# Feed-forward products of a two-block transformer kernel: seven quarter-size products for eight, with the weight sums on GpSimd

## The chip, the cores and the metric

The kernel runs on one core of a Trainium2 chip. The metric is the device time of one execution, in microseconds (us); smaller is better. A core has five engines with a queue of instructions each: TensorE (PE in the profile; its weight loads are listed apart as PEld), VectorE (DVE), ScalarE (ACT), GpSimd (POOL) and SyncE (SP), which here issues all DMAs. All data is fp32. Semaphores order the engines.

## The reference, cut to what matters

A first block (a hybrid of a recurrence and attention) is followed by a second block of two layers. Each layer ends with a feed-forward part, and that part alone is changed:

```python
DEPTH_2 = 2; N_META = 16; D_FF = 2816         # D_MODEL = 1024, SEQ = 256
h = concatenate([meta, x])                    # 272 tokens
for l in range(DEPTH_2):
    ...                                       # projections, attention, recurrence, convolution
    h = h + merged @ w_out[l]
    f = rms_norm_2(h, ffn_norm_g[l])
    a = silu(f @ w_ffn_gate[l]) * (f @ w_ffn_up[l])
    h = h + a @ w_ffn_down[l]
return h[:, N_META:]
```

Layer 0 computes 272 tokens in it, layer 1 the 256 that are returned.

## The kernel before, in words

Activations stand transposed: features on the 128 partitions, tokens along the free dimension. A tile of 128 features x 272 tokens is one unit of work. The residual `H` has `KD` = 8 such tiles, the hidden layer `FA` has `FT` = 22.

**Weights** come from DRAM in slots of 1 MB (128 partitions x 2048 numbers) into a ring of `RING` = 4. SP waits in `slot_free` until the slot that stood there has been used, then issues one DMA (`sync_layers`). `LSTREAM` gives the order of the slots of a layer: from `FF_S` = 54 on 22 slots in pairs (a gate slot and an up slot, each with two output tiles of 128 columns for all eight k), then from `DN_S` = 76 on 11 slots of the down matrix (two k tiles for all eight outputs each).

**TensorE** (`tensor_layers`) does 22 rounds, each a gate tile (L617) and an up tile (L625) of eight products with 272 (256) moving columns. PSUM banks 0 and 1 take the gates, 2 and 3 the ups. The first round works on `GH`, which is not yet normed, so that TensorE need not wait for the norm: its sum is taken by one product with ones (L443), ScalarE makes the root, and VectorE scales the results of the first two rounds, and writes the normed `NT` (L1073) for the other rounds. Then come 11 slots of down products (L636), which gather in eight banks over all slots. The last waits, `gate_kept` and `up_kept` at `FT`, stand ahead of the first down product.

**ScalarE** takes silu of a gate bank into `SG` (L818), **VectorE** multiplies it with the up bank into `FA` (L1079), and adds the down banks to `H` (L1082). **GpSimd** has no part in the layers of the second block; its last work is in the first block (L1443, L1456).

In the profile an fp32 product is two pairs of a weight load and a matmul, so that a tile of eight products is listed as x16; in a list of the program's order it is x8.

Each engine has its own queue, written in the program's order; there is no scheduler.

## Time and profile before

| | |
|---|---|
| median of 3 runs | 1852.68 us (1852.0 to 1853.68) |
| span of the profiled execution, first to last instruction | 1851.9 us |
| TensorE busy | 1808.0 us, 98% |
| VectorE, ScalarE, GpSimd busy | 738.4, 482.3, 115.9 us |
| mean granted TensorE clock | 0.988 of full speed |
| DMA | 225.20 MB, 122 GB/s in the mean |
| feed-forward part of layer 0, second product tile to last product | 969.51 to 1208.68 us |
| feed-forward part of layer 1, the same | 1623.58 to 1848.86 us |

The span is what this document reckons with; the median of the runs lies 0.8 us above it. A row of the chain of waits gives the start of a piece, its length, the engine and line on which the time passed, and how many instructions it covers; a row of a timeline gives start, length from the first start to the last end, and count, and in square brackets the idle time before it and what ended it. A row of the grouped view has the count, then busy time and mean duration of one, then idle time.

### The profile page before, as it was taken

The numbers are of one execution on the slowest core, as the hardware profiler recorded it, in microseconds if no ns is written. First come the engines' busy times: TensorE is split into PE (matmuls) and PEld (weight loads), VectorE is DVE, ScalarE is ACT, GpSimd is POOL, SyncE is SP. The second block draws the span as 40 slices with busy tenths as digits, with TensorE's granted clock in tenths as the row PEclk, the third lists the DMA queues.
The fourth block names the chain that finished last, engine by engine and source line by source line (L and its number), as shares of the span: only waits on it lengthen the run. The fifth ranks groups of instructions, "written<-read, shape, count | busy, mean of one in ns | idle before, by whom it ended". The sixth has DMA issues, their size and how long they took to land.

```text
span 1851.9 us, 28212 instructions
## 1 busy us (share of the span) xinstructions
PE 1808.0 (98%) x11966; PEld 1430.8 (77%) x11966; DVE 738.4 (40%) x1599; ACT 482.3 (26%) x1036; POOL 115.9 (6%) x133
## 2 busy tenths in 40 slices
PE   8999998999999999999999999999999999999999
PEld 3344654889877888888878888878888888888888
DVE  1233625556356958574211000048667563110000
ACT  2112236344343135642020000051237321110000
POOL 0000600465100000000000000000000000000000
PEclk9999999799899999999999999999999999999999
DMA  8412310000234434333333334443334334433352
GB/s 313 163 46 68 114 46 1 3 4 4 104 132 155 137 129 143 126 126 114 137 137 136 137 137 159 144 152 137 137 136 140 134 114 159 139 143 150 137 182 91
DMA packets 33213, 225.20 MB, mean 122 GB/s; under 512 B 4672, under 2 KB 6080, under 8 KB 6336
## 3 DMA queue, kind: packets, MB, share of 16 engines
q1 hardware_dynamic: 33088, 223.40, 34.0%
q8 instruction: 95, 1.56, 0.3%
q14 instruction: 30, 0.25, 0.0%
HBM read 222.34 MB, written 1.05 MB: 121 GB/s over the span
## 4 chain that ended last, share of the span: by engine, by line
PE 92%; DVE 3%; ACT 2%; SPq 1%; issue 1%; DVEq 0%; DMA 0%; POOL 0%; ACTq 0%
PE PS L457 25%; PE PS L598 12%; PE PS L1695 9%; PE PS L636 8%; PE PS L625 8%; PE PS L617 8%; PE PS L1201 2%; PE PS L1214 2%; PE PS L1634 2%; PE PS L1788 1%; PE PS L470 1%; PE PS L571 1%; SPq L1602 1%; PE PS L540 1%; PE PS L552 1%
## 5 line engine op out<-in xcount | busy, mean ns | idle before, releaser
L457 PE MATMUL PS<-arena,ring 128*128 128x272 f32 (+1 forms) x2176 | 498.1, 389 | 0.0
L457 PEld LDWEIGHTS PS<-arena,ring 128*128 128x128 f32 x2176 | 411.2, 190 | 77.2 <-issue 1.4
L598 PE MATMUL PS<-arena,ring 128*128 128x272 f32 (+1 forms) x1024 | 229.5, 386 | 2.1 <-DVE arena L1059 2.1
L598 PEld LDWEIGHTS PS<-arena,ring 128*128 128x128 f32 x1024 | 194.2, 190 | 36.0 <-DVE arena L1059 2.9
L851 DVE SCALAR_TENSOR_TENSOR arena<-arena,par 128x272 f32<-128x272 f32 (+1 forms) x480 | 214.8, 488 | 16.4 <-issue 0.9
L617 PE MATMUL PS<-arena,ring 128*128 128x272 f32 (+1 forms) x704 | 163.8, 386 | 0.0
L625 PE MATMUL PS<-arena,ring 128*128 128x272 f32 (+1 forms) x704 | 163.8, 386 | 0.0
L1695 PE MATMUL PS<-arena,ring 128*128 128x512 f32 (+2 forms) x448 | 158.2, 514 | 1.7 <-DVEq L1992 1.7
L636 PE MATMUL PS<-arena,ring 128*128 128x272 f32 (+1 forms) x704 | 157.1, 386 | 1.1 <-issue 1.1
L636 PEld LDWEIGHTS PS<-arena,ring 128*128 128x128 f32 x704 | 133.6, 190 | 24.7 <-issue 1.9
L617 PEld LDWEIGHTS PS<-arena,ring 128*128 128x128 f32 x704 | 133.8, 190 | 22.9
L625 PEld LDWEIGHTS PS<-arena,ring 128*128 128x128 f32 x704 | 133.8, 190 | 22.9
L1695 PEld LDWEIGHTS PS<-arena,ring 128*128 128x128 f32 (+1 forms) x448 | 84.0, 189 | 75.0 <-issue 69.5
L653 ACT ACTIVATE arena<-PS 128x272 f32<-128x272 f32 (+1 forms) x144 | 55.6, 392 | 323.8 <-PE PS L457 313.8
L1079 DVE TENSOR_TENSOR arena<-PS,arena 128x272 f32<-128x272 f32 (+1 forms) x44 | 19.0, 433 | 266.8 <-PE PS L625 266.5
L818 ACT ACTIVATE arena<-PS 128x272 f32<-128x272 f32 (+1 forms) x40 | 15.6, 390 | 268.2 <-PE PS L617 268.2
L1082 DVE TENSOR_TENSOR H<-H,PS 128x272 f32<-128x272 f32 (+1 forms) x16 | 6.9, 430 | 151.4 <-PE PS L636 151.4
L1634 PE MATMUL PS<-ring,smalls 128*2 128x256 f32 x192 | 45.0, 390 | 9.0 <-DMA ring<-stream_dram 9.0
L1456 POOL TENSOR_TENSOR ring<-arena,H 128x256 f32<-128x256 f32 x64 | 45.8, 742 | 87.9 <-ACT arena L1375 87.8
L1214 PE MATMUL PS<-arena,ring 64*64 64x32 f32 x1280 | 50.9, 228 | 0.3 <-issue 0.3
L1214 PEld LDWEIGHTS PS<-arena,ring 64*64 64x64 f32 x1280 | 47.0, 145 | 3.3 <-issue 2.1
L1057 DVE TENSOR_TENSOR arena<-PS,arena 128x272 f32<-128x272 f32 (+1 forms) x32 | 13.9, 433 | 80.3 <-PE PS L598 80.3
(323 smaller groups left out, 1777.4 us busy)
## 6 DMA issues: line engine op xcount, KB each, us to landing
ring<-stream_dram SPq DMA_DIRECT2D x207, 1024.0 KB, 4.8
arena<-x_dram SPq DMA_DIRECT2D x1, 2048.0 KB, 11.5
cst<-const_dram SPq DMA_DIRECT2D x1, 1080.0 KB, 7.6
out_dram<-H SPq DMA_DIRECT2D x4, 256.0 KB, 2.1
cst<-const_dram SPq DMA_DIRECT2D x1, 912.0 KB, 17.2
arena<-stream_dram SPq DMA_DIRECT2D x1, 512.0 KB, 7.1
par<-param_dram SPq DMA_DIRECT2D x2, 177.0 KB, 10.8
c<-const_dram SPq DMA_DIRECT2D x1, 128.0 KB, 2.2
```

The lines of the kernel that those rows point to most:

```text
L457: last = mm(PS[:, (m + f) % 4, nw], lslot(l, n, KD, 256)[:, k, P * f:P * f + P], NT[:, k, nw], start=k == 0, stop=k == KD - 1)
L598: last = mm(PS[:, i % 4, NQ], lslot(l, n, KD, 256)[:, k, P * (i % 2):P * (i % 2) + P], src[:, k, NQ], start=k == 0, stop=k == KD - 1)
L617: last = mm(PS[:, f, NQ], lslot(l, n, KD, 256)[:, k, P * f:P * f + P], src[:, k, NQ], start=k == 0, stop=k == KD - 1)
L625: last = mm(PS[:, 2 + f, NQ], lslot(l, n + 1, KD, 256)[:, k, P * f:P * f + P], src[:, k, NQ], start=k == 0, stop=k == KD - 1)
L636: last = mm(PS[:, f, NQ], w[:, k, P * f:P * f + P], FA[:, 2 * i + k, NQ], start=i == 0 and k == 0, stop=i == FT // 2 - 1 and k == 1)
L653: a(out, PS[:, m % 4, nw] if src is None else src, func, **more).then_inc(L["kept"], 1)
L851: stt(CVG[:, c, NQ], CVA[:, c, j + Q0:j + T2], dw_w[l][:, c, j:j + 1], CVG[:, c, NQ], ALU.mult, ALU.add)
L1201: last = mm(PS[halves(h), 4 * d, 32 * q:32 * q + 32], XL[l - 1][halves(h), d, q, :], columns(ZW[halves(h), n % 2, d, 0, q, :], l, GROWN[d] ...
L1214: last = mm(PS[halves(h), 4 * d, 256 + 32 * q:288 + 32 * q], ZW[halves(h), n % 2, d, 1, q, :], P1[halves(h), d, 32 * q:32 * q + 32], start ...
L1456: tt(XL[l - 1][:, d], AS[:, d], over(level_mask(d, l), 4), ALU.mult).then_inc(S["xl_ready"], 1)
L1634: last = mm(PS[0:2, n % 4, 0:256], SC[:, k, :], weights(n, KD, 256)[:, k, :], start=k == 0, stop=k == KD - 1)
L1695: last = mm(out, weights(n, KD, 256)[:, k, P * f:P * f + rows], HT[:, k, lo:T1], start=k == 0, stop=k == KD - 1)
```

## The change

The feed-forward products, but for the first gate and up pair of tiles, go over to Strassen's scheme in the form with seven products and fifteen sums. A slot is seen as four k pairs x (even, odd k) x (first, second 128 columns): four quarters a11, a12, a21, a22 of 4 x 128 columns each, and the tokens are halved (136 + 136, or 128 + 128). Each of the seven products has four k steps with half the tokens: 28 products of 136 columns for a slot, where 16 of 272 stood.

- GpSimd makes four sums of the quarters of each slot (`weight_sums`, into one of four `WS`): TensorE needs them from the third of the seven products on.
- The sums over tokens: of `NT` by VectorE once per layer (`TN`), of `FA` by GpSimd, a pair of tiles at a time (`TF`).
- ScalarE copies the first product out of PSUM (`CA`), VectorE puts the seven together (`combine`, four instructions), ScalarE takes silu of four gate quarters at once, and VectorE multiplies them with four up quarters into two tiles of `FA` after each second slot.
- 20 slots (`QUADS`) of gate and up, then 12 slots for the down matrix: for each of four pairs of output tiles (`fp`) three slots of 4, 4 and 3 k pairs. Each of those comes by two DMAs of up to 512 KB, whose rows in DRAM are 1 KB long.
- The seven results lie in three banks, and two sets of three banks alternate.

The diff, cut to its core:

```diff
-                elif FF_S <= i < DN_S:
-                    sp.wait_ge(L["up_made"], B["up_made"] + 2 * ((i - FF_S) // 2) + 2)
+                elif FF_S <= i < FF_S + 2:
+                    sp.wait_ge(L["up_made"], B["up_made"] + 2)
+                elif FF_S + 2 <= i < DN_S:
+                    sp.wait_ge(L["quad_part"], B["quad_part"] + 3 * (i - FF_S - 1))
                 elif i >= DN_S:
-                    sp.wait_ge(L["down_used"], B["down_used"] + i - DN_S + 1)
+                    down_wait(sp, l, i - DN_S)
...
+        def regions(nth, n):
+            first, second, third = ((5, 6, 7), (1, 2, 3))[nth % 2]
+            return ([PS[:, first, n * i:n * i + n] for i in range(3)] + [PS[:, second, n * i:n * i + n] for i in range(2)]
+                    + [PS[:, third, n * i:n * i + n] for i in range(2)])
...
+        def down_slot(s):
+            fp, i = divmod(s, 3)
+            return fp, range(4 * i, min(4 * i + 4, FT // 2))
+        def down_wait(engine, l, s):
+            if s % 3 < 2:
+                engine.wait_ge(L["down_used"], BASE[l]["down_used"] + 2 * (s // 3) + s % 3 + 1)
+            else:
+                engine.wait_ge(L["fold_made"], BASE[l]["fold_made"] + s + 1)
+        def quarters(l, n):
+            pairs = 4 if n < DN_S else len(down_slot(n - DN_S)[1])
+            w = lslot(l, n, 4, 2, 2, P)[:, 0:pairs]
+            return w[:, :, 0, 0, :], w[:, :, 1, 0, :], w[:, :, 0, 1, :], w[:, :, 1, 1, :]
...
+                if i < DN_S:
+                    sp.dma_start(ring[:, n % RING, :], w2_h[l, LSTREAM[i]]).then_inc(slot_in[n % RING], 16)
+                else:
+                    fp, ks = down_slot(i - DN_S)
+                    to = ring[:, n % RING, 0:512 * len(ks)].rearrange("p (k e c) -> p k e c", e=2, c=256)
+                    of = w2_h[l, DN_S + ks[0]:DN_S + ks[-1] + 1].rearrange("k p (e c) -> p k e c", e=2)
+                    cols = slice(256 * fp, 256 * fp + 256)
+                    sp.dma_start(to[:, :, 0, :], of[:, :, 0, cols]).then_inc(slot_in[n % RING], 16)
+                    sp.dma_start(to[:, :, 1, :], of[:, :, 1, cols]).then_inc(down_in[n % RING], 16)
...
-            pe.wait_ge(L["gate_kept"], B["gate_kept"] + FT)
-            pe.wait_ge(L["up_kept"], B["up_kept"] + FT)
-
-            for i in range(FT // 2):
-                lslot_wait(pe, l, DN_S + i)
-                w = lslot(l, DN_S + i, 2, D)
-                for f in range(KD):
-                    for k in range(2):
-                        last = mm(PS[:, f, NQ], w[:, k, P * f:P * f + P], FA[:, 2 * i + k, NQ],
-                                  start=i == 0 and k == 0, stop=i == FT // 2 - 1 and k == 1)
-                    if i == FT // 2 - 1:
-                        last.then_inc(L["down_made"], 1)
-                if i < FT // 2 - 1:
+            n0, n1 = token_halves(l)
+            nh = n0.stop - n0.start
+            def products(nth, w, sums, even, odd, ts):
+                a11, a12, _, a22 = w
+                a, c, b, g, e, h, d = regions(nth, nh)
+                return ((a, a11, even, n0), (b, a12, odd, n0), (c, sums[1], ts[1], None), (g, sums[0], ts[0], None),
+                        (e, sums[2], ts[2], None), (h, sums[3], odd, n1), (d, a22, ts[3], None))
+            for j in range(QUADS):
+                n = FF_S + 2 + j
+                lslot_wait(pe, l, n)
+                if j >= 2:
+                    pe.wait_ge(L["quad_read"], B["quad_read"] + j - 1)
+                if j == 0:
+                    pe.wait_ge(L["normed"], B["normed"] + 2 * KD)
+                    pe.wait_ge(L["root"], B["root"] + 2)
+                if j == 1:
+                    pe.wait_ge(L["gate_kept"], B["gate_kept"] + 2)
+                    pe.wait_ge(L["up_kept"], B["up_kept"] + 2)
+                made = products(j, quarters(l, n), [WS[j % 4][:, i] for i in range(4)], NT[:, 0::2, :], NT[:, 1::2, :],
+                                [TN[:, i, :, 0:nh] for i in range(4)])
+                for r, (out, w, src, tokens) in enumerate(made):
+                    if r == 2:
+                        if j == 0:
+                            pe.wait_ge(L["halves_made"], B["halves_made"] + 1)
+                        pe.wait_ge(L["slot_sums"], B["slot_sums"] + j + 1)
+                    for k in range(4):
+                        last = mm(out, w[:, k], src[:, k] if tokens is None else src[:, k, tokens], start=k == 0, stop=k == 3)
+                    if r in (2, 4, 6):
+                        last.then_inc(L["quad_part"], 1)
+            for s in range(DOWNS):
+                fp, ks = down_slot(s)
+                lslot_wait(pe, l, DN_S + s)
+                if fp < 2 and ks[0] == 0:
+                    pe.wait_ge(L["quad_read"], B["quad_read"] + QUADS - 1 + fp)
+                if fp >= 2 and ks[0] == 0:
+                    pe.wait_ge(L["h_added"], B["h_added"] + 2 * (fp - 1))
+                if fp == 0:
+                    pe.wait_ge(L["fa_made"], B["fa_made"] + ks[-1])
+                made = products(fp, quarters(l, DN_S + s), [WS[s % 4][:, i] for i in range(4)], FA[:, 0::2, :],
+                                FA[:, 1::2, :], [TF[:, i, :, 0:nh] for i in range(4)])
+                for r, (out, w, src, tokens) in enumerate(made):
+                    if r == 2:
+                        pe.wait_ge(L["slot_sums"], B["slot_sums"] + QUADS + s + 1)
+                        if fp == 0:
+                            pe.wait_ge(L["fa_halves"], B["fa_halves"] + ks[-1] + 1)
+                    for i, k in enumerate(ks):
+                        last = mm(out, w[:, i], src[:, k] if tokens is None else src[:, k, tokens],
+                                  start=k == 0 and r in (0, 3, 5), stop=k == 10 and r in (2, 4, 6))
+                    if ks[-1] == 10 and r in (2, 4, 6):
+                        last.then_inc(L["fold_made"], 1)
+                if s % 3 < 2:
                     last.then_inc(L["down_used"], 1)
...
+            for j in range(QUADS):
+                act.wait_ge(L["quad_part"], B["quad_part"] + 3 * j + 1)
+                a(CA[:, j % 2, 0:nh], regions(j, nh)[0], ACT.Copy).then_inc(L["quad_copied"], 1)
+                if j % 2 == 0:
+                    act.wait_ge(L["quad_read"], B["quad_read"] + j + 1)
+                    a(SGH[:, :, 0:nh], GR[:, 1:5, 0:nh], ACT.Silu).then_inc(L["silu_kept"], 1)
...
+        def weight_sums(e, w, to):
+            a11, a12, a21, a22 = w
+            to = to[:, :, 0:a11.shape[1]]
+            e.tensor_tensor(to[:, 0], a21, a22, ALU.add)
+            e.tensor_tensor(to[:, 2], a11, a21, ALU.subtract)
+            e.drain()
+            e.tensor_tensor(to[:, 1], to[:, 0], a11, ALU.subtract)
+            e.drain()
+            return e.tensor_tensor(to[:, 3], a12, to[:, 1], ALU.subtract)
+        def token_sums(e, even, odd, to, n0, n1):
+            nh = n0.stop - n0.start
+            to = to[..., 0:nh]
+            e.tensor_tensor(to[:, 0], even[..., n1], even[..., n0], ALU.subtract)
+            e.tensor_tensor(to[:, 2], odd[..., n1], even[..., n1], ALU.subtract)
+            e.drain()
+            e.tensor_tensor(to[:, 1], odd[..., n1], to[:, 0], ALU.subtract)
+            e.drain()
+            return e.tensor_tensor(to[:, 3], odd[..., n0], to[:, 1], ALU.subtract)
...
+                    dr()
+                    x = NT.rearrange("p (k e) t -> p k e t", e=2)
+                    token_sums(v, x[:, :, 0], x[:, :, 1], TN, n0, n1).then_inc(L["halves_made"], 1)
...
+            def combine(nth, to, copied, made):
+                cb, ge, hd = sums_of(nth, nh)
+                to, u = to[:, :, 0:nh], UU[:, :, 0:nh]
+                dr()
+                dve.wait_ge(*copied)
+                tt(to[:, 0:2], cb, over(CA[:, nth % 2, 0:nh], 2), ALU.add)
+                dr()
+                dve.wait_ge(made[0], made[1] + 2)
+                tt(u, ge, over(to[:, 0], 2), ALU.add)
+                dr()
+                tt(to[:, 4], ge[:, 0], u[:, 1], ALU.add)
+                dve.wait_ge(made[0], made[1] + 3)
+                return tt(to[:, 2:4], hd, u, ALU.add)
+            for j in range(QUADS):
+                combine(j, UP if j % 2 else GR, (L["quad_copied"], B["quad_copied"] + j + 1),
+                        (L["quad_part"], B["quad_part"] + 3 * j)).then_inc(L["quad_read"], 1)
+                if j % 2:
                     dr()
-                tt(FA[:, i, NQ], PS[:, 2 + i % 2, NQ], SG[:, i % 2, NQ], ALU.mult).then_inc(L["up_kept"], 1)
-            for f in range(KD):
-                dve.wait_ge(L["down_made"], B["down_made"] + f + 1)
-                tt(H[:, f, NQ], H[:, f, NQ], PS[:, f, NQ], ALU.add).then_inc(L["h_added"], 1)
-
-
+                    dve.wait_ge(L["silu_kept"], B["silu_kept"] + j // 2 + 1)
+                    tt(FA[:, j + 1:j + 3, NQ].rearrange("p f (n t) -> p f n t", n=2),
+                       UP[:, 1:5, 0:nh].rearrange("p (f n) t -> p f n t", f=2),
+                       SGH[:, :, 0:nh].rearrange("p (f n) t -> p f n t", f=2), ALU.mult).then_inc(L["fa_made"], 1)
+            for fp in range(4):
+                combine(fp, GR, (L["fold_copied"], B["fold_copied"] + fp + 1), (L["fold_made"], B["fold_made"] + 3 * fp))
+                dr()
+                for f in range(2):
+                    h = H[:, 2 * fp + f, NQ].rearrange("p (n t) -> p n t", n=2)
+                    tt(h, h, GR[:, 1 + 2 * f:3 + 2 * f, 0:nh], ALU.add).then_inc(L["h_added"], 1)
+        def pool_layers(pool, l):
+            g = nc.gpsimd
+            B = BASE[l]
+            NQ = slice(first_token(l), T2)
+            n0, n1 = token_halves(l)
+            def slot_sums(j):
+                lslot_wait(pool, l, FF_S + 2 + j)
+                if 4 <= j < QUADS + 4:
+                    pool.wait_ge(L["quad_part"], B["quad_part"] + 3 * (j - 3))
+                elif j >= 4:
+                    down_wait(pool, l, j - QUADS - 4)
+                weight_sums(g, quarters(l, FF_S + 2 + j), WS[j % 4]).then_inc(L["slot_sums"], 1)
+            pool.wait_ge(L["gate_made"], B["gate_made"] + 1)
+            for j in range(QUADS + DOWNS):
+                slot_sums(j)
+                if j % 2 and j < QUADS + 2:
+                    p = j // 2
+                    if p:
+                        pool.wait_ge(L["fa_made"], B["fa_made"] + p)
+                    else:
+                        pool.wait_ge(L["up_kept"], B["up_kept"] + 2)
+                    token_sums(g, FA[:, 2 * p, :], FA[:, 2 * p + 1, :], TF[:, :, p], n0, n1).then_inc(L["fa_halves"], 1)
+                    g.drain()
...
```

TensorE's queue, layer 0, from the second round made in the old way on; before (gates L617, ups L625, down L636):

```order
L617 MATMUL PS<-arena,ring 128x272 x8
L625 MATMUL PS<-arena,ring 128x272 x8
L617 MATMUL PS<-arena,ring 128x272 x8
L625 MATMUL PS<-arena,ring 128x272 x8
L617 MATMUL PS<-arena,ring 128x272 x8
L625 MATMUL PS<-arena,ring 128x272 x8
```

And now (L672 and L678 the gate and up tile of the second round, L711 the slots; a weight operand without `ring` is one of GpSimd's sums):

```order
L672 MATMUL PS<-arena,ring 128x272 x8
L678 MATMUL PS<-arena,ring 128x272 x8
L711 MATMUL PS<-arena,ring 128x136 x8
L711 MATMUL PS<-arena 128x136 x16
L711 MATMUL PS<-arena,ring 128x136 x12
L711 MATMUL PS<-arena 128x136 x16
L711 MATMUL PS<-arena,ring 128x136 x12
```

What moved: 28 products of 136 columns stand for 16 of 272 in a slot. Two of the seven products of a slot come from the ring (x8), the next four from the sums (x16), the last from the ring again; x12 is the last of one slot and the first two of the next.

GpSimd's queue, layer 0, two slots and one pair of `FA` tiles (L932 to L937 the four sums over a slot, L943 to L948 over tokens); in the queue before nothing stands here:

```order
L932 TENSOR_TENSOR arena<-ring 128x512
L933 TENSOR_TENSOR arena<-ring 128x512
L935 TENSOR_TENSOR arena<-arena,ring 128x512
L937 TENSOR_TENSOR arena<-ring,arena 128x512
L932 TENSOR_TENSOR arena<-ring 128x512
L933 TENSOR_TENSOR arena<-ring 128x512
L935 TENSOR_TENSOR arena<-arena,ring 128x512
L937 TENSOR_TENSOR arena<-ring,arena 128x512
L943 TENSOR_TENSOR arena<-arena 128x136
L944 TENSOR_TENSOR arena<-arena 128x136
L946 TENSOR_TENSOR arena<-arena 128x136
L948 TENSOR_TENSOR arena<-arena 128x136
```

What moved: this group of twelve comes ten times in a layer (for slots 0 to 19), then the slots of the down matrix follow, with one more token group after the second of them.

VectorE's queue at the start of the feed-forward part of layer 0; before (L1070 scales a gate, L1073 makes `NT`, L1079 makes a tile of `FA`):

```order
L1070 TENSOR_TENSOR arena<-PS,arena 128x272
L1073 TENSOR_TENSOR arena<-arena 128x272 x8
L1077 TENSOR_TENSOR arena<-arena 128x272
L1079 TENSOR_TENSOR arena<-PS,arena 128x272
L1070 TENSOR_TENSOR arena<-PS,arena 128x272
```

And now (L1193 for L1070, L1196 for L1073, L943 to L948 the token sums `TN`):

```order
L1193 TENSOR_TENSOR arena<-PS,arena 128x272
L1196 TENSOR_TENSOR arena<-arena 128x272 x8
L943 TENSOR_TENSOR arena<-arena 128x544
L944 TENSOR_TENSOR arena<-arena 128x544
L946 TENSOR_TENSOR arena<-arena 128x544
L948 TENSOR_TENSOR arena<-arena 128x544
L1202 TENSOR_TENSOR arena<-arena 128x272
L1204 TENSOR_TENSOR arena<-PS,arena 128x272
```

What moved: four instructions of 544 elements stand between the normed tiles and the first tile of `FA`.

## Rows read from the trace of the kernel before

**Rows 1.** The page: busy us (share of the span) and instructions of each engine

```profile
PE 1808.0 (98%) x11966; PEld 1430.8 (77%) x11966; DVE 738.4 (40%) x1599; ACT 482.3 (26%) x1036; POOL 115.9 (6%) x133
```

**Rows 2.** Stretches: length; PE, PEld, DVE, ACT, POOL busy (count); clock, DMA share, GB/s

```profile
969.51:1129.83 160.32, 159.74 (x698) 132.16 (x697) 14.19 (x34) 12.28 (x26) 0.00 (x0) 1.00 0.36 134
1129.83:1208.68 78.85, 78.83 (x344) 65.01 (x343) 3.08 (x7) 5.47 (x13) 0.00 (x0) 1.00 0.44 155
...
1772.64:1848.86 76.22, 76.21 (x352) 66.76 (x352) 2.95 (x7) 0.00 (x0) 0.00 (x0) 1.00 0.38 133
```

**Rows 3.** Chain of waits, feed-forward part: start, length, what, count

```profile
964.76 0.02 issue
...
969.51 3.67 PE PS L625 x16
...
1627.03 3.45 PE PS L617 x16
...
1772.07 0.56 issue
```

**Rows 4.** Chain, products of 144 and of mixed columns; a group of weight loads

```profile
767.73 0.98 PE PS L552 x8
...
836.40 3.98 PE PS L571 x24
...
L571 PEld LDWEIGHTS PS<-arena 128*128 128x128 f32 x96 | 15.3, 190 | 2.4 <-ACT arena L794 1.2
```

**Rows 5.** GpSimd's instructions grouped by shape

```profile
L1443 POOL TENSOR_TENSOR arena<-arena 128x512 f32<-128x512 f32 x16 | 20.0, 1271 | 72.9 <-ACT arena L1123 72.9
...
L1934 POOL TENSOR_TENSOR H<-cst 128x64 f32<-128x64 f32 x12 | 3.4, 321 | 21.4 <-DMA cst<-const_dram 21.4
```

**Rows 6.** Timeline of GpSimd: with a drain between, and back to back

```profile
220.24 2.35 POOL L1954 TENSOR_TENSOR arena<-arena 128x1024 f32<-128x1024 f32 x1
222.74 1.90 POOL L1956 TENSOR_TENSOR arena<-arena,par 128x1024 f32<-128x1024 f32 x1
...
371.50 2.78 POOL L1456 TENSOR_TENSOR ring<-arena,H 128x256 f32<-128x256 f32 x4
...
450.97 2.50 POOL L1443 TENSOR_TENSOR arena<-arena 128x512 f32<-128x512 f32 x2 [2.15 <-ACT arena L1123]
```

**Rows 7.** Timelines, VectorE beside GpSimd

```profile
181.74 1.57 DVE L2006 SCALAR_TENSOR_TENSOR arena<-arena,par 128x510 f32<-128x510 f32 x2
...
185.99 4.83 DVE L2006 SCALAR_TENSOR_TENSOR arena<-arena,par 128x510 f32<-128x510 f32 x1
185.60 4.67 POOL L1943 TENSOR_TENSOR arena<-arena 64x2048 f32<-64x2048 f32 x1 [160.14 <-DVE arena L2019]
...
190.33 4.88 POOL L1943 TENSOR_TENSOR arena<-arena 64x2048 f32<-64x2048 f32 x1
...
200.19 4.60 POOL L1943 TENSOR_TENSOR arena<-arena 64x2048 f32<-64x2048 f32 x1
...
371.88 0.75 DVE L1512 TENSOR_TENSOR arena<-PS,cst 128x256 f32<-128x256 f32 x2
```

**Rows 8.** Timeline, VectorE at the start of layer 0's feed-forward part

```profile
967.49 0.73 DVE L824 TENSOR_TENSOR arena<-arena 128x544 f32<-128x544 f32 x1
...
971.85 0.44 DVE L1070 TENSOR_TENSOR arena<-PS,arena 128x272 f32<-128x272 f32 x1 [3.11 <-ACT arena L659]
972.20 2.89 DVE L1073 TENSOR_TENSOR arena<-arena 128x272 f32<-128x272 f32 x8
```

**Rows 9.** Chain of waits behind the last product of each layer

```profile
1208.70 0.45 DVE H L1082
...
1848.88 0.42 DVE H L1082
```

**Rows 10.** DMA issues: KB each, us from issue to landing

```profile
ring<-stream_dram SPq DMA_DIRECT2D x207, 1024.0 KB, 4.8
...
out_dram<-H SPq DMA_DIRECT2D x4, 256.0 KB, 2.1
```

92 lines of the change are left out of this document (53 added, 39 removed).

## The prediction

> **What bounds the kernel now.** I read the page first: TensorE is busy for 98% of the span, no other engine for more than 40% [rows 1]. Then three stretches of the feed-forward parts, since only those change (gate and up of layer 0, down of layer 0, down of layer 1): TensorE is busy for 159.7 of 160.3, 78.8 of 78.9 and 76.2 of 76.2 us, the clock is 1.00 (2.4 GHz), VectorE works 14, 3 and 3 us, GpSimd not at all, and the ring's transfers keep up [rows 2]. So TensorE's instruction stream is the time here, and a product less is time less, until something else has to be waited for. The chain of waits gives the price of a tile: x16 in 3.67 us in layer 0 (272 columns), 3.45 us in layer 1 (256 columns) [rows 3], which is 229 and 216 ns for one instruction.
>
> **TensorE, the gain.** What would one of 136 (layer 0) or 128 columns (layer 1) cost? Products of 144 columns, each with a weight load of its own, take 0.98 us for eight, 122.5 ns each; from 256 to 272 columns a column costs 0.83 ns, so I take 115.8 and 109.2 ns. The danger is the weight load, of which there are now nearly twice as many per microsecond; one lasts 190 ns. But 24 instructions of 272, 192 and 64 columns (eight of each) take 3.98 us; at 229 and 162.5 ns the first two kinds make 3.13 us, which leaves 106 ns for one of 64 columns [rows 4]. So loads follow each other at about 106 ns, and with 128 or more columns they are just covered. Bounds from the rows: 109 to 190 ns; I take the low end, because the 144-column row is the nearest.
> - Gate and up, 20 slots a layer, 32 instructions before and 28 x 2 = 56 now: 40 x 3.67 = 146.7 us to 20 x 56 x 115.8 ns = 129.7 us, minus 17.0. Layer 1: 138.1 to 122.3 us, minus 15.8.
> - Down: 352 instructions (80.7 and 76.2 us by rows 2 and 3) to 7 x 11 x 4 x 2 = 616 (71.3 and 67.3 us), minus 9.4 and 8.9.
> - The stop ahead of the down products, 0.56 us in layer 1 [rows 3] and as much in layer 0, goes, since the first down slot needs only old tiles: minus 1.1.
> Together minus 52.2 us, if TensorE never waits.
>
> **GpSimd, the new load.** A two-input instruction of 512 elements lasts 1.27 us, one of 64 lasts 0.32 us [rows 5], hence 2.12 ns an element, 0.47 us for 136 and 0.46 us for 128. Two of 512 back to back take 2.50 us, and a drain between two leaves 0.15 us (222.59 to 222.74) [rows 6]. The sums of a slot: 2.50 + 0.15 + 1.27 + 0.15 + 1.27 = 5.34 us. The token sums of a pair of tiles: 0.92 + 0.15 + 0.47 + 0.15 + 0.47 + 0.15 = 2.3 us. Two slots and one pair: 13.0 us, in layer 1 12.9 us. TensorE needs 2 x 56 instructions for the same: 12.97 us in layer 0, 12.23 us in layer 1. That is nearly a draw, so what GpSimd loses beside VectorE counts.
>
> VectorE and GpSimd get in each other's way. A VectorE instruction with two inputs from SBUF, 0.75 us when alone (two in 1.57 us), lasted 4.83 us from 185.99 on: it ended 0.55 us after the GpSimd instruction that had started at 185.60. The next GpSimd instruction took 4.88 us where one alone took 4.60 us, 0.28 us more. Two VectorE instructions that read PSUM, beside GpSimd's run at 371.50, kept to 0.75 us [rows 6, 7]. So one blocks only with two SBUF inputs, passes at GpSimd's next instruction boundary, and costs GpSimd about 0.28 us. In a pair of slots only the product of silu and up (544 elements) is of that kind: `combine` reads PSUM. I take 0.28 us from the row; ends are 0 and its whole duration, 0.73 us for 544 elements [rows 8]. GpSimd's pair: 13.27 and 13.2 us.
>
> The Trainium skill (SBUF — State Buffer, section "SBUF: two separate sides") says that the two engines' common port pair is an exclusive lock for the whole instruction, in one case if VectorE has two SBUF inputs. The trace agrees on the 4.83 us; of the other direction it shows 0.28 us, where the rule read literally asks for 0.73 us. By that the sum below would be 1823 us.
>
> *Start of the part.* Layer 0: the products before the part end at 964.76 [rows 3], the first gate tile 3.67 us behind them, at 968.4; there GpSimd starts with slots 0 and 1, 2 x 5.34 us. VectorE starts on the eight `NT` instructions at 972.20 [rows 8], all with two SBUF inputs, so about one passes per GpSimd instruction: six until GpSimd is done, at 968.4 + 10.7 + 6 x 0.28 = 980.9 (each costs GpSimd 0.28). Then two more (0.7) and the four token sums of 0.73 us (2.9): 984.5. TensorE is at slot 0 at 980.51 (969.51 + 3 x 3.67) and needs the token sums two products (1.85 us) later: a wait of 2.1 us. Layer 1, the same way with its first gate tile done at 1622.5: sums at 1638.5, needed at 1627.03 + 2 x 3.45 + 1.75 = 1635.7: 2.8 us. Together plus 5.0; ends 0 (GpSimd doesn't block) and 9.
>
> *Steady state, layer 0.* VectorE needs 2.8 us behind 984.5 for the first two `FA` tiles; GpSimd's token sums, then slot 2: ready at 995.0. TensorE wants it at 984.5 + 40 x 0.1158 + 6.49 + 1.85 = 997.5. A lead of 2.5 us shrinks by 13.27 - 12.97 = 0.3 in each of nine pairs: plus 0.2. Layer 1: lead 1.8 us, nine times 13.2 - 12.23 = 0.99: plus 7.1. In the down slots GpSimd has no token sums but one and is ahead again (5.34 a slot against 6.49 and 6.1). Bounds: 0, and 24 us for a pair of 14.2 us (one more instruction's lock and 0.05 us a wait).
>
> *Tails.* Behind the last product of a layer now come an instruction of `combine`, a drain and two additions to `H` (0.44 + 0.06 + 0.44 + 0.36 = 1.3 us) in place of one of 0.42 to 0.45 [rows 9]: plus 0.9 for each of the two layers, 1.8.
>
> *Costs of nothing.* VectorE's combine, about 2.4 us per slot, lies beside 6.1 to 6.5 us of TensorE, in another bank set, and with it ScalarE. A ring slot lands 4.8 us after its issue [rows 10], and is asked for three slots (18 us) ahead of its use. The down slots come in rows of 1 KB; the output, with pieces of 1 KB in SBUF, took 2.1 us for 256 KB, so 8.4 us for 1 MB at worst: hidden, as 18 + 1.8 - 5.3 us are free.
>
> **Sum.** 1851.9 - 52.2 + 5.0 + 7.3 + 1.8 = 1813.8; the median of the runs lies 0.8 above the span: 1815 us.
>
> **Rivals.**
> - *Everything hides* (GpSimd instructions a little shorter, or VectorE passing freely): only the tails are left, 1802 us. For it: the draw in layer 0. Against: 12.9 us is over 12.23 before any lock.
> - *GpSimd dearer*: a pair of 14.2 us makes 8.6 + 15.9 us of the steady terms in place of 7.3: 1832 us. For it: no row shows GpSimd summing for 150 us on end, nor a subtraction, nor reading the ring while TensorE does. Against: its durations hardly scatter (all of 512 at 1.27).
> - *The weight load shows; slower.* If at 128 and 136 columns a load is partly bare, each of 3472 instructions pays. The break-even is (52.2 - 6.8) / 3472 = 13 ns over the mean of 112.7 ns, at 125.7 ns. Midway between 116 and the 190 ns of one load, at 153 ns, TensorE needs 531 us for what took 441.7 us, GpSimd is hidden: 1948 us. For it: 190 ns is more than 116. Against: 106 ns at 64 columns [rows 4]. The Trainium skill (TensorE: Matmul & The Clock Gate, section "Back-to-back issue gap") speaks for it: in streams of load and matmul it has 81 ns at N=128 where the matmul alone has 56. In this trace the products of 144 columns show nothing of it; none of 128 with real weights is there.
> - *The down slots land late*, above 14 us each for the 1 KB rows: over 20 down slots each us more costs up to 20 us. Against: rows 10.
>
> **Numbers.** My forecast 50% (1807 to 1822), all hidden 12%, GpSimd dearer 25%, bare load 7%, late transfers 3%, the rest 3%. Range 1802 to 1840. About 0.2% (4 us) is what a measurement tells from no change; faster 0.89, same 0.02, slower 0.09.
>
> **What would show it.** Intervals of 116 and 109 ns inside a slot; TensorE's idle time ended by GpSimd (L937), none or little in layer 0, some 0.8 us per pair in layer 1 from about the fourth slot on; 2 to 3 us of idle at each slot 0, ended by VectorE; GpSimd's pairs at 13.2 us, its 512-element sums at 1.27 us; VectorE's `NT` instructions stretched to over 1 us. The forecast is wrong if an interval is over 120 ns, or if TensorE's idle time in the two parts is under 5 or over 25 us.

## The result, and the profile after

| | before | after |
|---|---|---|
| median of the runs beside each other | 1852.34 us (1848.95 to 1853.68, 4 runs) | 1821.41 us (1816.6 to 1822.21, 4 runs) |
| span of the profiled execution | 1851.9 us | 1820.4 us |
| second product tile to last product, layer 0 | 239.17 us | 215.48 us |
| the same, layer 1 | 225.28 us | 212.13 us |
| last product of layer 0 to the second product tile of layer 1 | 414.90 us | 418.41 us |
| last product to the end | 3.0 us | 3.9 us |

The ratio is 0.982, interval 0.980 to 0.984; 1815 us was forecast, with 1802 to 1840 as the range. The spans differ by 31.5 us: −23.69 and −13.15 in the two parts, +3.51 between them, +0.84 at the end, and +0.99 ahead of the first part (970.50 in place of 969.51 us). No work of any engine up to there is changed, in this kernel or in the ones below, and yet their profiled executions reach the second up tile as much as 15 us apart (961.78 and 977.27 us). So what follows goes by the lengths of the parts, which the same kernel repeated within 0.2 us in a later execution, and not by the medians alone.

The table counts as the chain of waits does. A timeline has the first start of a tile 0.16 us ahead of the end of the tile before. Layer 0's part goes from one start to the next tile's start and is the same by both. Layer 1's part ends with an end, so it is 0.16 us longer by the timelines: 212.29 us for this kernel. The experiments below are read from timelines and go by that number; the repeat had 215.62 and 212.42 us.

The page, beside [rows 1]:

```profile
PE 1766.2 (97%) x13454; PEld 1451.2 (80%) x13454; DVE 844.8 (46%) x1779; ACT 492.4 (27%) x1064; POOL 479.7 (26%) x477
```

TensorE is busy for 41.8 us less with 1488 instructions more. GpSimd's 26% over the span hides that in the quad slots it works nearly without pause: it is busy for 119.9 of the 130 us from 990 us on.

The start of layer 0's part, TensorE and then VectorE and GpSimd (start, length from first start to last end, count; in brackets the idle time before and what ended it):

```profile
970.34 3.83 PE L678 MATMUL PS<-arena,ring 128*128 128x272 f32 x16
...
981.71 2.09 PE L711 MATMUL PS<-arena,ring 128*128 128x136 f32 x16 [0.21 <-issue]
984.72 3.97 PE L711 MATMUL PS<-arena 128*128 128x136 f32 x32 [0.91 <-DVE arena L948]
988.53 2.94 PE L711 MATMUL PS<-arena,ring 128*128 128x136 f32 x24
991.31 3.87 PE L711 MATMUL PS<-arena 128*128 128x136 f32 x32
...
997.79 0.39 PE L711 MATMUL PS<-arena 128*128 128x136 f32 x2
```

```profile
973.19 8.42 DVE L1196 TENSOR_TENSOR arena<-arena 128x272 f32<-128x272 f32 x8
...
983.94 0.72 DVE L948 TENSOR_TENSOR arena<-arena 128x544 f32<-128x544 f32 x1
```

```profile
976.30 1.46 POOL L933 TENSOR_TENSOR arena<-ring 128x512 f32<-128x512 f32 x1
...
979.33 1.28 POOL L937 TENSOR_TENSOR arena<-ring,arena 128x512 f32<-128x512 f32 x1
```

The eight `NT` instructions, 2.89 us before [rows 8], take 8.42 us beside GpSimd, which is done with its eight at 980.6; the token sums are ready at 984.7, and TensorE waits for them. From 991.31 to 997.79, one slot, there are 56 instructions in 6.48 us, 115.7 ns each (115.8 over longer stretches).

The steady state of layer 1:

```profile
1624.75 3.74 PE L711 MATMUL PS<-arena 128*128 128x128 f32 x32
1628.32 2.84 PE L711 MATMUL PS<-arena,ring 128*128 128x128 f32 x24
1631.00 3.74 PE L711 MATMUL PS<-arena 128*128 128x128 f32 x32
...
1682.19 3.84 PE L711 MATMUL PS<-arena 128*128 128x128 f32 x32 [0.84 <-POOL arena L937]
...
1695.60 3.84 PE L711 MATMUL PS<-arena 128*128 128x128 f32 x32 [0.64 <-POOL arena L937]
```

```profile
1689.71 1.27 POOL L932 TENSOR_TENSOR arena<-ring 128x512 f32<-128x512 f32 x1 [0.22 <-PE PS L711]
...
1693.77 1.78 POOL L937 TENSOR_TENSOR arena<-ring,arena 128x512 f32<-128x512 f32 x1
...
1703.07 1.28 POOL L932 TENSOR_TENSOR arena<-ring 128x512 f32<-128x512 f32 x1 [0.22 <-PE PS L711]
```

A slot takes TensorE 6.25 us (1624.75 to 1631.00), 111.6 ns an instruction and not 109.2. GpSimd's pair lasts 13.36 us (1689.71 to 1703.07). The waits stand 13.4 us apart, so GpSimd sets the pace from there on. One of its sums per pair lasts 1.78 in place of 1.27 us: the one during which VectorE multiplies silu and up (L1227).

Between the layers, TensorE, then ScalarE and VectorE:

```profile
1185.82 3.99 PE L532 MATMUL PS<-arena,ring 128*128 128x256 f32 x16
1192.07 1.28 PE L505 MATMUL PS<-arena,c 128*128 128x272 f32 x2 [2.26 <-DVE arena L926]
1193.14 11.46 PE L532 MATMUL PS<-arena,ring 128*128 128x256 f32 x48
1204.44 3.83 PE L546 MATMUL PS<-arena,ring 128*72 128x272 f32 x16
```

```profile
1183.24 0.28 ACT L918 ACTIVATE arena<-PS 128x136 f32<-128x136 f32 x1 [17.55 <-PE PS L732]
1183.42 0.51 ACT L757 ACTIVATE arena<-H,par 128x272 f32<-128x272 f32 x1
...
1188.96 0.42 ACT L758 ACTIVATE arena<-H 128x272 f32<-128x272 f32 x1
```

```profile
1186.54 0.79 DVE L1235 TENSOR_TENSOR H<-H,arena 128x272 f32<-128x272 f32 x2
...
1189.41 1.29 DVE L922 TENSOR_TENSOR arena<-arena 128x1088 f32<-128x1088 f32 x1 [2.08 <-ACT arena L758]
```

Layer 1's first tile starts at 1185.82, and the last product of layer 0 ends at 1185.98. ScalarE's sixteen activations for the next layer, which before ran while the down products did, all stand behind its copy L918 in its queue and begin at 1183.42, though six of the eight tiles of `H` had long been complete. So the sum of squares (L922) starts 3.59 us behind the start of that first tile, and TensorE stands 2.26 us in front of the norm product L505. Then comes a lower clock (columns: length, busy us with counts, granted clock, DMA):

```profile
1189.00:1192.00 3.00, 0.78 (x3) 0.30 (x2) 2.44 (x4) 2.92 (x6) 0.00 (x0) 0.94 0.36 153
1192.00:1196.00 4.00, 3.93 (x11) 3.24 (x12) 1.97 (x15) 3.01 (x6) 0.00 (x0) 0.62 0.00 0
1196.00:1200.00 4.00, 4.00 (x20) 3.51 (x19) 3.85 (x13) 0.38 (x1) 0.00 (x0) 1.00 0.32 72
```

### The profile page after: what moved, and what is told of

Its sections match the earlier page's. It is cut to its first block, busy times and chain, and to the rows that moved or that the text cites. A ratio compares the mean times of both kernels' runs of the same rounds, so it can differ in the third digit from the quotient of the medians.

```text
span 1820.4 us, 32164 instructions
## 1 busy us (share of the span) xinstructions
PE 1766.2 (97%) x13454; PEld 1451.2 (80%) x13454; DVE 844.8 (46%) x1779; ACT 492.4 (27%) x1064; POOL 479.7 (26%) x477
## 3 DMA queue, kind: packets, MB, share of 16 engines
HBM read 222.34 MB, written 1.05 MB: 123 GB/s over the span
## 4 chain that ended last, share of the span: by engine, by line
PE 77%; POOLq 7%; POOL 6%; DVE 3%; issue 3%; ACT 2%; SPq 1%; DMA 1%; DVEq 0%; ACTq 0%
PE PS L519 26%; PE PS L660 12%; PE PS L1873 9%; PE PS L732 7%; POOL arena L937 3%; POOLq L936 3%; POOLq L934 3%; PE PS L1379 2%; PE PS L711 2%; PE PS L1392 2%; PE PS L1812 2%; POOL arena L932 1%; POOL arena L933 1%; PE PS L532 1%; PE PS L1966 1%
## 5 line engine op out<-in xcount | busy, mean ns | idle before, releaser
L519 PE MATMUL PS<-arena,ring 128*128 128x272 f32 (+1 forms) x2176 | 498.1, 389 | 0.0
L519 PEld LDWEIGHTS PS<-arena,ring 128*128 128x128 f32 x2176 | 411.2, 190 | 77.2 <-issue 1.4
L932 POOL TENSOR_TENSOR arena<-ring 128x512 f32<-128x512 f32 (+1 forms) x64 | 83.3, 1302 | 929.9 <-PE PS L672 925.1
L660 PE MATMUL PS<-arena,ring 128*128 128x272 f32 (+1 forms) x1024 | 229.5, 386 | 2.1 <-DVE arena L1181 2.1
L660 PEld LDWEIGHTS PS<-arena,ring 128*128 128x128 f32 x1024 | 194.2, 190 | 36.0 <-DVE arena L1181 2.9
L711 PE MATMUL PS<-arena 128*128 128x136 f32 (+1 forms) x1280 | 153.0, 278 | 5.8 <-POOL arena L937 4.0
L711 PEld LDWEIGHTS PS<-arena 128*128 128x128 f32 x1280 | 148.6, 191 | 7.4 <-POOL arena L937 5.2
L747 ACT ACTIVATE arena<-PS 128x272 f32<-128x272 f32 (+1 forms) x144 | 55.7, 393 | 324.5 <-PE PS L519 313.7
L711 PE MATMUL PS<-arena,ring 128*128 128x136 f32 (+1 forms) x960 | 116.2, 277 | 1.0 <-issue 1.0
L711 PEld LDWEIGHTS PS<-arena,ring 128*128 128x128 f32 x960 | 112.4, 191 | 1.7 <-issue 1.7
L1212 DVE TENSOR_TENSOR arena<-PS,arena 128x272 f32<-128x272 f32 (+1 forms) x48 | 20.8, 433 | 186.5 <-ACT arena L918 104.2
L937 POOL TENSOR_TENSOR arena<-ring,arena 128x512 f32<-128x512 f32 (+1 forms) x64 | 83.1, 1298 | 9.7 <-issue 0.4
L732 PE MATMUL PS<-arena 128*128 128x136 f32 (+1 forms) x704 | 84.2, 277 | 1.3 <-POOL arena L937 1.3
L732 PEld LDWEIGHTS PS<-arena 128*128 128x128 f32 x704 | 81.9, 191 | 1.6 <-POOL arena L937 1.6
L933 POOL TENSOR_TENSOR arena<-ring 128x512 f32<-128x512 f32 (+1 forms) x64 | 82.7, 1291 | 0.0
L935 POOL TENSOR_TENSOR arena<-arena,ring 128x512 f32<-128x512 f32 (+1 forms) x64 | 80.1, 1251 | 9.1
L732 PE MATMUL PS<-arena,ring 128*128 128x136 f32 (+1 forms) x528 | 64.3, 277 | 0.0
L732 PEld LDWEIGHTS PS<-arena,ring 128*128 128x128 f32 x528 | 62.1, 191 | 0.0
```

Of the source, the lines that this page charges most:

```text
L519: last = mm(PS[:, (m + f) % 4, nw], lslot(l, n, KD, 256)[:, k, P * f:P * f + P], NT[:, k, nw], start=k == 0, stop=k == KD - 1)
L660: last = mm(PS[:, i % 4, NQ], lslot(l, n, KD, 256)[:, k, P * (i % 2):P * (i % 2) + P], src[:, k, NQ], start=k == 0, stop=k == KD - 1)
L711: last = mm(out, w[:, k], src[:, k] if tokens is None else src[:, k, tokens], start=k == 0, stop=k == 3)
L732: last = mm(out, w[:, i], src[:, k] if tokens is None else src[:, k, tokens], start=k == 0 and r in (0, 3, 5), stop=k == 10 and r in (2, 4 ...
L747: a(out, PS[:, m % 4, nw] if src is None else src, func, **more).then_inc(L["kept"], 1)
L932: e.tensor_tensor(to[:, 0], a21, a22, ALU.add)
```

## The experiments

Theory after the result: products are as cheap as forecast but for 2.4 ns at 128 columns; what is lost is waits on GpSimd (start of each part, steady pace, more for the lock than forecast) and the seam between the layers (counted from the first product of the next layer, L532, to its first L546). Rivals: GpSimd's own slowness without VectorE, a TensorE interval that the load sets, and no queue effect at the seam. All edits are to the kernel as changed; the ratios in brackets are to the kernel before, run beside each. Medians taken at other times differ by some us for one and the same kernel (1821.41 and 1818.26 us for the one as changed), so a gain is read from the parts and the seam.

### GpSimd starts later on slot 1

```diff
             for j in range(QUADS + DOWNS):
+                if j == 1:
+                    pool.wait_ge(L["halves_made"], B["halves_made"] + 1)
                 slot_sums(j)
```

> Edit: GpSimd makes the sums of slot 0, then waits until VectorE has made the token sums TN, and only then goes on with slot 1. Theory: the 1.5 us (layer 0) and 2.0 us (layer 1) that TensorE idles around slot 0 in the changed kernel come from VectorE's NT and TN instructions, each of which waits for a GpSimd instruction to end (8 NT took 8.42 us, against 2.89 before). With GpSimd out of the way after slot 0 the NT take about 4 us, TN is there before TensorE asks, and the time falls by 3.5 us, to 1818. The sums of slot 1 are then ready at about 985.7, needed at 989.7. Rival: the wait only moves to slot 1 or 2, because GpSimd is late from then on: no gain, 1821, with TensorE idle ended by L937 early in each layer.

Measured: 1815.43 us (ratio 0.979, 0.975 to 0.984).

```profile
969.52 4.13 DVE L1196 TENSOR_TENSOR arena<-arena 128x272 f32<-128x272 f32 x8
...
977.67 2.02 PE L711 MATMUL PS<-arena,ring 128*128 128x136 f32 x16
979.52 3.87 PE L711 MATMUL PS<-arena 128*128 128x136 f32 x32
```

No idle time is left at slot 0 in either layer; from the second up tile to the sums it is 12.85 us in place of 14.38 (979.52 − 966.67, 984.72 − 970.34), and 2.0 us less in layer 1. That is the cost of VectorE's and GpSimd's meeting, shown by taking it away. But layer 1's whole part is only 1.2 us shorter (211.07 against 212.29), and layer 0's is 1.3 us shorter (214.21): with GpSimd started later, layer 1 has seven waits on its sums and not six.

The seam shows something else. The wait ahead of the norm product is the same, but the clock stays at 1.00 behind it, and the seam takes 17.17 in place of 18.62 us (1180.88 to 1198.05):

```profile
1187.13 0.73 PE L505 MATMUL PS<-arena,c 128*128 128x272 f32 x2 [2.26 <-DVE arena L926]
1187.69 10.52 PE L532 MATMUL PS<-arena,ring 128*128 128x256 f32 x48
```

### VectorE's product without its second input from SBUF

```diff
                     tt(FA[:, j + 1:j + 3, NQ]...,
-                       UP[:, 1:5, 0:nh]...,
+                       over(PS[:, 0, 0:nh], 4)...,
                        SGH[:, :, 0:nh]..., ALU.mult)
```

The up values are left out of `FA`: what stands in PSUM bank 0 is multiplied in their place.

> Edit: VectorE's product of silu and up reads one of its two inputs from PSUM (bank 0) in place of the up values in SBUF, so that FA is made without the up values; sizes and order are unchanged. Theory: what stretches one of GpSimd's instructions per pair of slots from 1.27 to 1.78 us is this product with its two SBUF inputs. Without it a pair of slots takes GpSimd 12.9 us in place of 13.4 us, TensorE's idle time in layer 1 (5.5 us over six waits) falls to about 1.5 us and that in layer 0 (1.55) to nothing: 5 us less, 1816. Rival A: GpSimd is stretched by any VectorE instruction, or by TensorE reading the ring: pairs stay at 13.4 us, time 1821. Rival B (the lock costs only what I predicted, 0.28 us): pairs at 13.1, time 1819.

Measured: 1814.96 us (0.978, 0.975 to 0.981).

```profile
1675.18 1.28 POOL L932 TENSOR_TENSOR arena<-ring 128x512 f32<-128x512 f32 x1 [0.22 <-issue]
...
1688.16 1.27 POOL L932 TENSOR_TENSOR arena<-ring 128x512 f32<-128x512 f32 x1 [0.22 <-issue]
```

The pair is 12.98 us, no sum of GpSimd in the quad slots lasts over 1.33 us, and of the six waits in layer 1 two of 0.2 us are left; its part is 208.08 us (−4.2). So 0.4 us of each pair is VectorE's doing. The rival, that GpSimd is slow by itself, falls: alone it is the 12.9 us that the sum of its rows gave.

### The norm product one tile later

```diff
-                if m == (0 if l else 1):
+                if m == 1:
                     norm_sums(0, 5, NW)
```

> Edit: in layer 1 the product of the norm sum stands behind the second QI tile in place of the first (in layer 0 it stood there already). Theory: between the layers TensorE now idles 2.3 us ahead of the norm product, because ScalarE's 16 activations for the next layer all stand behind its copy of the last fold; the granted clock then falls to 0.62 in the 4 us behind it. With one more tile ahead of the norm product there is no idle time, the clock stays up, and the time falls by 2.3 + 1.2 = 3.5 us, to 1818. Rival: the root comes later, and TensorE waits for the normed tiles at the KI product in its place: no gain, 1821.

Measured: 1815.97 us (0.979, 0.976 to 0.982).

```profile
1179.37 7.44 PE L532 MATMUL PS<-arena,ring 128*128 128x256 f32 x32
1186.65 0.62 PE L505 MATMUL PS<-arena,c 128*128 128x272 f32 x2
1187.11 7.07 PE L532 MATMUL PS<-arena,ring 128*128 128x256 f32 x32
1194.01 3.83 PE L546 MATMUL PS<-arena,ring 128*72 128x272 f32 x16
```

The seam, first L532 to L546, is 14.64 in place of 18.62 us; nothing waits, and the clock stays at 1.00. In the kernel before it was 14.71 us (1208.92 to 1223.63). Of the 4.0 us, 2.5 hung on one product's place. The other 1.5 are the lower clock, which the same wait did not bring in the run with the late start (17.17 us).

### GpSimd made dearer

```diff
                     token_sums(g, FA[:, 2 * p, :], FA[:, 2 * p + 1, :], TF[:, :, p], n0, n1)...
+                    g.tensor_tensor(cut(21976, 4, P), WS[0][:, 0], WS[0][:, 0], ALU.add)
                     g.drain()
```

> Edit: one more GpSimd instruction of 512 elements and a drain behind the token sums of each pair of slots (22 in all, output unused). Theory: GpSimd sets the pace; its pair grows by 1.27 + 0.15 = 1.42 us to 14.8, and each of the nine pairs between slot 2 and the down slots passes it on to TensorE in both layers: 2 x 9 x 1.4 = 25 us more, 1846, TensorE's idle time ended by L937 in every second slot from the first pairs on, 1.85 us a pair in layer 0 and 2.3 in layer 1. Rival: GpSimd is not what TensorE waits for (a ring slot or the PSUM banks are, and GpSimd's end is only the last of several): under 8 us more.

Measured: 1843.55 us (0.994, 0.991 to 0.996; eight runs).

```profile
PE PS L711 <- POOL arena L937: 21.4, 16, 1.6
```

```profile
1054.87 1.04 POOL L1263 TENSOR_TENSOR arena<-arena 128x512 f32<-128x512 f32 x1 [0.16 <-issue]
```

(The first row is of the view of waits: total us, times, longest.) One instruction of 1.04 us and its drain made the pair 14.5 us (1054.87 to 1069.39); from the second up tile to the norm product layer 0 takes 11.8 us more (233.55 against 221.73), layer 1's part 11.4 us more (223.67), 23 in all. The extra instruction took 1.04 and not the expected 1.27 us, and so the loss is 22 and not 25 us by the medians. Some seven tenths of the gain of the change go by 1.1 us more per pair of slots: GpSimd is the bound of the quad slots, with no slack in layer 0 either.

### Fewer columns

```diff
-    last = mm(out, w[:, k], src[:, k] if tokens is None else src[:, k, tokens], ...)
+    at = 0 if tokens is None else tokens.start
+    last = mm(out[:, 0:(64, 112)[l]], w[:, k], src[:, k, at:at + (64, 112)[l]], ...)
```

The products of the remaining tokens are left out.

> The products of the quad and down slots run on fewer columns: 64 in layer 0 (136 before the edit), 112 in layer 1 (128 before). The remaining tokens' products are left out, everything else stays. Inside one group of 32 products the interval is read from the group's busy time. Theory A (a 32-bit weight load with its own product has a floor that does not depend on the columns, near the 107 to 112 ns that small products and 128 columns showed): 105 to 112 ns for both widths, so groups of 32 of about 3.4 to 3.6 us in both layers. Theory B (the interval is columns / 1.2 plus 2.5 ns all the way down): 56 ns (1.8 us) for 64 columns, 96 ns (3.1 us) for 112. Theory C (floor at the 111.6 ns of 128 columns exactly, since the load sets it): 3.57 us or more for both. The pair of slots stays at GpSimd's 13.4 us in both layers in every theory, with the idle time of TensorE in front of every second slot grown to 1.2 us or more in layer 0.

Measured: 1989.73 us, one execution. Layer 1 (112 columns), then layer 0 (64 columns):

```profile
1804.69 3.74 PE L712 MATMUL PS<-arena 128*128 128x112 f32 x32
1808.26 2.84 PE L712 MATMUL PS<-arena,ring 128*128 128x112 f32 x24
...
988.18 7.09 PE L712 MATMUL PS<-arena 128*128 128x64 f32 x32 [1.04 <-DVE arena L950]
...
1012.13 7.04 PE L712 MATMUL PS<-arena 128*128 128x64 f32 x32
1018.95 5.33 PE L712 MATMUL PS<-arena,ring 128*128 128x64 f32 x24
1024.07 7.03 PE L712 MATMUL PS<-arena 128*128 128x64 f32 x32
```

```profile
1000.00:1200.00 200.00, 200.00 (x939) 200.00 (x939) 32.97 (x75) 10.06 (x25) 98.83 (x99) 0.50 0.24 87
```

In layer 1 112 columns take exactly what 128 took, 3.74 and 2.84 us: between these two widths the interval of 111.6 ns no longer depends on the columns, so it is the load with its product that sets it, and theory B falls for that width.

What happened in layer 0 no theory had. The granted clock was 1.00 up to the usual wait for the token sums, 1.04 us here, and 0.50 (1.2 GHz) from the products behind it on (988.18 us). It stayed there for 367 us, as long as the products had 64 columns, although TensorE did not stand idle once in that time; it was 0.52 for another 5 us in which the products of 256 columns came back, and 1.00 behind them. The interval there is 213 ns (1012.13 to 1024.07 us, 56), half of which is 106.6: close to the 106 ns that the prediction had for 64 columns at the full clock, and not the 56 ns of theory B. The part lasted 381.4 in place of 215.5 us, and TensorE, not GpSimd, set its pace. What brought the clock down, the width or the wait, no run here separates: a wait of 0.91 us at the same place was followed by 1.00 with products of 136 columns, and one of 0.86 us in layer 1 of this same execution with 112. One execution does not show either whether it would fall again.

### VectorE makes the weight sums

```diff
+        BY_VECTOR = (2, ..., 19)
...
+                m = j + 2                     # behind combine(j)
+                if m in BY_VECTOR:
+                    ...
+                    weight_sums(v, quarters(l, FF_S + 2 + m), WS[m % 4]).then_inc(L["vec_sums"], 1)
...
-                slot_sums(j)
+                if j not in BY_VECTOR:
+                    slot_sums(j)
```

> VectorE makes the weight sums of slots 2 to 19, each behind its combination of slot j-2; GpSimd makes those of slots 0 and 1, the token sums and the down slots' sums. Theory A (what sets the steady pace now is GpSimd's 13.35 to 13.42 us for a pair; VectorE has 1.6 + 0.4 + 0.2 + 2.8 = about 5 us of work in a slot of 6.25 to 6.49): every wait of TensorE on sums inside the quad slots goes, 1.55 us in layer 0 and 5.5 us in layer 1; the waits at the start stay or grow to 2 to 3 us a layer, since NT still stands behind GpSimd; about 7 us less than the kernel with GpSimd alone, near 1814. Rival (VectorE comes to its sums only behind the evictions of slot j-2, so they are late): a wait of TensorE of 0.5 us or more in front of most quad slots, 10 us or more lost over 36 slots, slower than the kernel with GpSimd alone.

Measured: 1814.31 us (0.978, 0.975 to 0.981), beside 1818.26 us of the kernel as changed. In the view of waits not one on sums of slots is left, only those of the token sums at the start:

```profile
PE PS L719 <- DVE arena L956: 1.8, 2, 0.9
```

The parts are 213.72 and 206.48 us, 1.9 and 5.9 less than in the kernel as changed beside it (215.62 and 212.42): theory A in size, though the medians lie only 4.0 us apart. VectorE, at 46% of the span, was the engine with room.

### Four edits at once

The two edits of the start and of the norm product, `BY_VECTOR = (5, 11, 17)` (behind the combination of slot j − 3), and on ScalarE:

```diff
             for fp in range(4):
+                if fp == 3 and l < LAYERS - 1:
+                    for k in range(6):
+                        next_gain(act, l + 1, k)
                 act.wait_ge(L["fold_made"], B["fold_made"] + 3 * fp + 1)
```

> Four edits at once: GpSimd's sums for slot 1 wait until the token sums of VectorE are made; VectorE makes the sums of slots 5, 11 and 17; the norm product of the next layer stands one tile later; ScalarE does six of the eight pairs of the next layer's activations ahead of its last copy. Theory: the waits at the start go (1.5 us in layer 0, 2.0 in layer 1), the waits on sums go (1.55 and 5.5), the seam between the layers is 4 us shorter, in all 14.5 us less than the kernel as changed: layer 0's part 212.4 us from its second up tile to its last product where that had 215.5, layer 1's 205 where it had 212.2, near 1807. Rival (VectorE's sums collide with GpSimd's through their shared lock, or make the combinations late): waits stay on the slots behind 5, 11 and 17, and 3 us or more of the gain are missing.

Measured: 1807.37 us (0.974, 0.971 to 0.978), 10.9 us less than the kernel as changed beside it.

```profile
PE PS L719 <- POOL arena L953: 0.7, 1, 0.7
```

The parts are 212.08 and 205.32 us and the seam is 14.28 us (1183.95 to 1198.23), as expected, which is 3.5, 7.1 and 4.6 us less than in the kernel as changed beside it. The medians show 10.9 of these 15.2 us, where 14.5 was expected; the execution shown reached its second up tile 7.0 us later than that of the kernel beside it (971.87 and 964.92 us). One wait of 0.68 us is left in both parts together. With that wait and its 0.1 us of a slower restart taken off, layer 1's part is 204.5 us. This has the lowest median of the versions that were run, 43.8 us under the kernel before beside it.

> The kernel as changed, once more, on the same chip as the two above, to set them against: every theory expects 0.982 of the kernel before, within 0.002, a layer 0 part of 215.5 us and a layer 1 part of 212.2.

That run gave 1818.26 us (0.982, 0.979 to 0.985), with the parts named above. Its seam was 18.86 us (1180.54 to 1199.40), with a granted clock of 0.59 behind the wait of 2.27 us.

### ScalarE's activations ahead of its last copy, alone

> Alone: ScalarE does the first six of the eight pairs of layer 1's gain and square activations ahead of its last copy of layer 0's folds, instead of behind it. In the kernel as changed VectorE's sum of the squares starts 3.59 us behind the last product of layer 0, and TensorE stands 2.26 us in front of the norm product. Theory (in-order ScalarE: ten of the sixteen activations are still to be done when H is complete): the sum of squares starts 2.8 us behind the last product, as where the norm product was moved too, and the wait of TensorE is 1.5 us; with the clock at 1.00 from there on the seam (last product to the KI tiles) lasts 16.4 us, with a fall of the clock as in the kernel as changed 18. Rival (VectorE's combination sets the time, ScalarE has slack): the wait stays at 2.2 to 2.3 us. The rest as in the kernel as changed, 1817 to 1820 us in all.

Measured: 1818.46 us (0.981, 0.977 to 0.985).

```profile
1187.12 3.62 PE L532 MATMUL PS<-arena,ring 128*128 128x256 f32 x16
1192.58 0.72 PE L505 MATMUL PS<-arena,c 128*128 128x272 f32 x2 [1.84 <-DVE arena L934]
...
1203.51 3.83 PE L546 MATMUL PS<-arena,ring 128*72 128x272 f32 x16
```

```profile
1189.92 1.29 DVE L930 TENSOR_TENSOR arena<-arena 128x1088 f32<-128x1088 f32 x1 [1.28 <-ACT arena L744]
```

The sum of squares starts 2.80 us behind the start of the first L532 tile, as expected, and the norm product 5.46 us behind it in place of 6.25. The seam is 16.39 us with the clock at 1.00 throughout, 0.8 us less than the 17.17 us at that clock without the edit. The wait is 1.84 and not 1.5 us, since the view ends the sixteen instructions ahead of it 0.4 us earlier here (3.62, not 3.99). ScalarE's queue is worth 0.8 us; the rival falls.

## Why the prediction was right, point by point

**The gain.** Without waits the parts should have been 239.17 − 17.0 − 9.4 − 0.55 = 212.2 us and 225.28 − 15.8 − 8.9 − 0.55 = 200.0 us. The version with four edits, which hardly waits, has 212.1 and, counted as the table does, 204.4. Layer 0 is right to 0.1 us. Layer 1 is 4.4 us short, of which 20 × 0.135 + 0.0024 × 616 = 4.2 us come from the interval, 111.6 ns for 109.2: the step that scaled from 256 to 128 columns at 0.83 ns a column. The prediction had set the floor of the load at 106 ns, from a sum over mixed products [rows 4]; with 112 columns it measured 111.6. The rival of the bare load thus held in kind at 128 columns, at 2.4 ns, far from its break-even of 13. The Trainium skill (TensorE: Matmul & The Clock Gate, "Back-to-back issue gap") has 81 ns for load and matmul at N=128 where the matmul alone has 56, a difference of 25 ns, and nothing of that size shows in these runs.

**The start.** Forecast 2.1 and 2.8 us, measured 1.5 and 2.0 by the start-late run. The mechanism was as told (`NT` 8.42 us, VectorE passing at GpSimd's boundaries); the size was 1.5 us too dear together (3.5 where the sum had 5.0).

**The lock.** Forecast 0.28 us a pair, measured 0.4 to 0.5 (1.78 against 1.27 us; a pair of 13.36 us, and 12.98 with it gone). It lies between the row that was chosen, 0.28, and the whole duration of VectorE's instruction, 0.69 us here (1693.73 on, beside the 1.78). The rule of the Trainium skill (SBUF — State Buffer, "SBUF: two separate sides"), that the one that comes second waits for the whole of the first, read literally asks for that whole duration; these runs show 0.4 to 0.5.

**The steady state.** GpSimd's pairs are 13.4 us in both layers, forecast 13.27 and 13.2. Layer 0 lost 215.48 − 212.08 − 1.5 = 1.9 us in place of 0.2; the run without the lock won 1.8 there. Layer 1 lost 212.29 − 204.5 − 2.0 = 5.8 in place of 7.1: TensorE's pair was 12.5 and not 12.23 us, so the slower product hid part of GpSimd's excess. Interval 4.2 too cheap, waits 2.1 too dear: the layer gained 13.15 us where 15.35 was forecast. The sign that the prediction had named, some 0.8 us of idle time per pair in layer 1 from about the fourth slot on, came later: six waits, 0.84 and then 0.64 us each, the first at 1682.19 us, ten slots in. The idle time of TensorE in the two parts together is 8.0 us, inside its bounds of 5 and 25.

**The tails.** At the end +0.84 us, as forecast (0.9). Between the layers the step failed: 0.9 us was forecast from VectorE's instructions alone, and it was 3.5. That step looked only at what VectorE adds behind the last product, and not at who waits behind it in which queue. Before, TensorE went from the last product to the norm product like this:

```profile
1208.92 3.69 PE L470 MATMUL PS<-arena,ring 128*128 128x256 f32 x16 [0.26 <-ACT arena L663]
1212.71 0.73 PE L443 MATMUL PS<-arena,c 128*128 128x272 f32 x2
```

The norm product stood 4.03 us behind the end of the last product (1208.68 to 1212.71) and stands 6.09 us behind it now (1185.98 to 1192.07), 2.1 us later. Of these, 0.9 is VectorE's tail (`H` complete 1.35 us behind the last product, 0.47 before) and 0.8 ScalarE's order (shown by the run with that edit alone). The rest, about 0.4 us, goes with two halves of `H` completing together, so that four activations and not two stand behind them (argued from the timelines, not tested). The other 1.45 us are the clock: the norm product and the 48 instructions behind it take 0.51 and 0.94 us longer than where the clock stayed at 1.00, as it did in four executions with the same wait. As far as these runs show, that is chance. Without the fall the seam would have cost 2.1 us against the 0.9 forecast. The seam's cost is gone wholly where no wait stands there.

**Costs of nothing.** Right: no wait on a slot of the ring is in the view. The halves of 512 KB of the down slots land in 4.0 us:

```profile
ring<-stream_dram SPq DMA_DIRECT2D x32, 512.0 KB, 4.0
```

In sum, the span was forecast at 1813.8 and came out at 1820.4: 0.9 us more in layer 0's part, 2.2 in layer 1's, 2.6 at the seam, 1.0 that lies ahead of all changed code, and 0.1 less at the end. That this is under 7 us is in part luck of sign: in layer 1 an interval 4.2 us too cheap stands against waits 2.1 us too dear.

## What to carry to other kernels

Count a scheme that trades products for sums by the engine that makes the sums, per slot and beside its neighbours, not by its share of the span: here GpSimd was busy for 26% of it and still set the pace, and three slots' sums in twenty moved to VectorE took 5.75 us off layer 1's part (211.07 to 205.32 us), nearly all that GpSimd's pace had cost there. Where the end of a layer is moved, go through the queue of every engine that works across it, and ask what stands behind the instruction that is now late. And when products get narrower, their price stops falling (here between 128 and 112 columns), and one must look at the granted clock before counting a gain.
